# First norm through diagonal products: scaling and turning of x in one step, the samples' root apart, the first two projection units one after the other

## What is computed

```python
def rmsnorm(x, g):
    xf = x.astype(jnp.float32)
    y = xf * lax.rsqrt(jnp.mean(xf * xf, axis=-1, keepdims=True) + RMS_EPS) * g.astype(jnp.float32)
    return y.astype(x.dtype)
...
ap = rmsnorm(hp, norm_mix[i])
asm = rmsnorm(hs, norm_mix[i])
q, k, v, qi, ki, wi = attn_project(ap, pos_p, w_attn_in[j])
```

## Time and profile before

| | |
|---|---|
| median of 3 runs | 620.13 us (619.17 to 621.24) |
| profiled execution, span from first to last instruction | 619.9 us |
| mean granted TensorE clock | 0.992 |
| busy: TensorE / VectorE / ScalarE / GpSimd | 95% / 74% / 59% / 38% |

### The profile page before, as it was taken

How to read it: one execution, slowest core, us unless ns; L and a number is a source line. 1 busy time by engine, 2 the same in 40 slices (tenths; PEclk the granted TensorE clock), 3 DMA queues, 4 the chain that set the end, 5 groups by cost and what they waited for, 6 DMA issues and landing times.

```text
span 619.9 us, 12865 instructions
## 1 busy us (share of the span) xinstructions
PE 591.2 (95%) x5069; PEld 509.9 (82%) x5069; DVE 458.3 (74%) x900; ACT 366.8 (59%) x620; POOL 238.1 (38%) x259
## 2 busy tenths in 40 slices
PE   7889997899999999999999999898999999999995
PEld 6778875888888888888888778776888888888885
DVE  4779998465787777888668785888877788775442
ACT  6784555566576556666565687655765566653322
POOL 4222226642345445542000497923454454420000
PEclk9999999799999999999999999999999999999999
DMA  9678578235867666778997752035676667778501
GB/s 262 189 180 202 162 222 255 85 103 155 293 192 211 193 192 198 202 217 234 261 266 216 211 171 70 1 110 157 194 212 189 197 198 199 225 224 234 151 6 70
DMA packets 205421, 113.29 MB, mean 183 GB/s; under 512 B 5561, under 2 KB 202217, under 8 KB 205337
## 3 DMA queue, kind: packets, MB, share of 16 engines
q1 hardware_dynamic: 203169, 106.33, 60.7%
q0 software_dynamic: 1680, 5.79, 2.8%
q10 hardware_dynamic: 512, 0.35, 0.2%
HBM read 108.83 MB, written 3.86 MB: 182 GB/s over the span
## 4 chain that ended last, share of the span: by engine, by line
PE 66%; DVE 14%; POOL 7%; ACT 5%; issue 4%; DMA 3%; SPq 1%; DVEq 0%; POOLq 0%; ACTq 0%
PE acc L1467 18%; PE acc L1470 18%; PE acc L1473 18%; DVE w_lo L962 5%; PE acc L1447 2%; DMA stage<-in_w_ffn_down 2%; ACT w_hi L591 2%; POOL area L1954 1%; PE acc L1479 1%; DVE area L1094 1%; POOL area L1950 1%; POOL area L1959 1%; PE acc L1614 1%; POOL rtail L1949 1%; PE acc L1616 1%
## 5 line engine op out<-in xcount | busy, mean ns | idle before, releaser
L1467 PE MATMUL acc<-aH,w_hi 128*128 128x264 f16 (+1 forms) x904 | 250.0, 277 | 1.7 <-DVE aL L971 1.6
L1470 PE MATMUL acc<-aL,w_hi 128*128 128x264 f16 (+1 forms) x904 | 249.7, 276 | 0.0
L1473 PE MATMUL acc<-aH,w_lo 128*128 128x264 f16 (+1 forms) x904 | 249.7, 276 | 0.0
L962 DVE SCALAR_TENSOR_TENSOR w_lo<-stage,w_hi 128x1024 f16<-128x1024 f32 (+1 forms) x155 | 204.2, 1321 | 40.3 <-ACT w_hi L591 39.9
L591 ACT ACTIVATE w_hi<-stage 128x1024 f16<-128x1024 f32 (+1 forms) x155 | 171.4, 1109 | 38.4 <-PE acc L1473 27.5
L1467 PE MATMUL acc<-zH,w_hi 128*128 128x264 f16 x384 | 106.0, 276 | 0.0
L1470 PE MATMUL acc<-zL,w_hi 128*128 128x264 f16 x384 | 106.0, 276 | 0.0
L1473 PE MATMUL acc<-zH,w_lo 128*128 128x264 f16 x384 | 106.0, 276 | 0.0
L1467 PEld LDWEIGHTS acc<-aH,w_hi 128*128 128x128 f16 (+1 forms) x904 | 88.6, 98 | 16.0 <-DVE aL L971 2.2
L1470 PEld LDWEIGHTS acc<-aL,w_hi 128*128 128x128 f16 (+1 forms) x904 | 90.1, 100 | 13.6
L1473 PEld LDWEIGHTS acc<-aH,w_lo 128*128 128x128 f16 (+1 forms) x904 | 90.1, 100 | 12.9
(11 more groups left out here) (407 smaller groups left out, 969.5 us busy)
## 6 DMA issues: line engine op xcount, KB each, us to landing
stage<-in_w_ffn_up SPq DMA_DIRECT2D x88, 512.0 KB, 4.7
stage<-in_w_ffn_down SPq DMA_DIRECT2D x32, 704.0 KB, 6.1
stage<-in_w_attn_in SPq DMA_DIRECT2D x22, 512.0 KB, 6.0
stage<-in_w_rec_in SPq DMA_DIRECT2D x16, 512.0 KB, 4.8
stage<-in_w_attn_out SPq DMA_DIRECT2D x8, 512.0 KB, 3.9
stage<-in_w_rec_out SPq DMA_DIRECT2D x8, 512.0 KB, 3.8
area<-in_w_attn_in SPq DMA_DIRECT2D x4, 512.0 KB, 5.3
area<-in_x_prompt SPq DMA_DIRECT2D x2, 512.0 KB, 4.9
```

The costliest lines, as they stand in the source:

```text
L962: v.scalar_tensor_tensor(low, stage[:, place_in_line(u) % 4, 0:n, 0:cols], WSCALE, high, ALU.mult, ALU.subtract).then_inc(lo_done, 1)
L1467: t_.matmul(out, high[:, c, :], xH[:, x0 + c, :], start=first and c == 0, stop=False)
L1470: t_.matmul(out, high[:, c, :], xL[:, x0 + c, :], start=False, stop=False)
L1473: ins = t_.matmul(out, low[:, c, :], xH[:, x0 + c, :], start=False, stop=last and c == n - 1)
```

## The change

The row factors are no longer multiplied into the tokens. VectorE builds a diagonal matrix of them (`rdiag`, now at the start, and no longer at step 16), and TensorE multiplies a block of tokens by it, which scales and turns in one product; the transposes are gone. The samples' root, reciprocal and diagonal come ahead of the prompt's. The loads of the norm weights go from GpSimd's queue to ScalarE's, the loads of the page table and `blkc` the other way, and GpSimd sets `ones` ahead of its loads. `aH` of the samples is written by VectorE. Units 0 and 1 run one after the other, and `hi(1)` and `lo(1)` come after all eight chunks. The four warming products stand between the samples' and the prompt's products.

```diff
@@ ScalarE
-            act.dma_start(pt8[:], a["page_table"]).then_inc(pt_in, 16)
+            for i, name in enumerate(("norm_mix", "norm_ffn")):
+                act.dma_start(nrow[16 * i:16 * i + 16, :], a[name].rearrange("k (c p) -> (k c) p", p=P)).then_inc(nrm_in, 16)
+            act.dma_start(nrow[32:40, :], a["norm_final"].rearrange("(c p) -> c p", p=P)).then_inc(nrm_in, 16)
...
+            act.wait_ge(ss_act, 1)
+            nc.scalar.activation(rms[:, 2:3], ss[:, 2:3], ACT.Sqrt, bias=epsc[:, 0:1], scale=1.0 / D).then_inc(s_root, 1)
...
+            act.wait_ge(g_turned, 1)
+            nc.scalar.copy(gcol[:], acc[:, 2, 0:5 * DC]).then_inc(x_kept, 1)
...
-            nc.scalar.activation(rms[:], ss[:], ACT.Sqrt, bias=epsc[:, 0:1], scale=1.0 / D).then_inc(rms_root, 1)
-            act.wait_ge(r0tok_done, 1)
-            nc.scalar.activation(xtok[:, 0, :], xtok[:, 0, :], ACT.Copy, scale=r0tok[:, 0:1]).then_inc(xn0, 1)
+            nc.scalar.activation(rms[:, 0:2], ss[:, 0:2], ACT.Sqrt, bias=epsc[:, 0:1], scale=1.0 / D).then_inc(rms_root, 1)
...
@@ VectorE
+            dve.wait_ge(s_root, 1)
+            v.reciprocal(r0tok[:, 2:3], rms[:, 2:3]).then_inc(r0tok_done, 1)
...
+            v.tensor_scalar(rdiag[:, 2, :], ident, r0tok[:, 2:3], None, ALU.mult).then_inc(s_diag, 1)
...
-            v.tensor_scalar(xsmp, xsmp, r0tok[0:NS, 2:3], None, ALU.mult).then_inc(xn1, 1)
-            v.tensor_scalar(xtok[:, 1, :], xtok[:, 1, :], r0tok[:, 1:2], None, ALU.mult).then_inc(xn1, 1)
...
+            v.tensor_copy(aH[:, :, TP:T], xg[:]).then_inc(xg_done, 1)
+            dve.wait_ge(rms_root, 1)
+            v.reciprocal(r0tok[:, 0:2], rms[:, 0:2]).then_inc(r0tok_done, 1)
+            dve.wait_ge(r0tok_done, 2)
+            for t in range(2):
+                v.tensor_scalar(rdiag[:, t, :], ident, r0tok[:, t:t + 1], None, ALU.mult).then_inc(rdiag_done, 1)
...
@@ TensorE
+            t_.transpose(acc[:, 2, 0:5 * DC], nrow, ident[0:5 * DC, 0:5 * DC]).then_inc(g_turned, 1)
+            pe.wait_ge(s_diag, 1)
             for c in range(DC):
-                ins = t_.transpose(acc[:, 3, NS * c:NS * (c + 1)], xsmp[:, c * P:(c + 1) * P], ident[0:NS, 0:NS])
+                ins = t_.matmul(acc[:, 3, NS * c:NS * (c + 1)], xsmp[:, c * P:(c + 1) * P], rdiag[0:NS, 2, 0:NS], start=True, stop=True)
             ins.then_inc(s_turned, 1)
+            keep_warm(acc[:, 0, 0:P], WARM // 4)
             for c in range(DC):
+                for t in range(2):
+                    pe.wait_ge(rdiag_done, t + 1)
+                    ins = t_.matmul(misc[:, c // 2, c % 2 * TP + t * P:c % 2 * TP + (t + 1) * P], xtok[:, t, c * P:(c + 1) * P],
+                                    rdiag[:, t, :], start=True, stop=True)
                 if c % 2:
                     ins.then_inc(x_turned, 1)
...
-            keep_warm(acc[:, 2, 0:P], 4)
...
+            unit(0, aH, aL, ready=a_ready(0))
+            unit(1, aH, aL)
@@ GpSimd
-            for i, name in enumerate(("norm_mix", "norm_ffn")):
-                pool.dma_start(nrow[16 * i:16 * i + 16, :], a[name].rearrange("k (c p) -> (k c) p", p=P)).then_inc(nrm_in, 16)
-            pool.dma_start(nrow[32:40, :], a["norm_final"].rearrange("(c p) -> c p", p=P)).then_inc(nrm_in, 16)
             g.memset(ss[:], 1.0)
             g.memset(epsc[:], EPS)
+            g.memset(ones[:], 1.0).then_inc(ones_set, 1)
...
+            pool.dma_start(pt8[:], a["page_table"]).then_inc(pt_in, 16)
             g.memset(rfin[:], 1.0)
-            g.memset(ones[:], 1.0).then_inc(ones_set, 1)
```

More of the change, by code:

```diff
@@ L375, in build @@
         ss_act, ss_dve, r0tok_done = sem("ss_act"), sem("ss_dve"), sem("r0tok_done")
-        xn0, xn1, s_turned, x_turned = sem("xn0"), sem("xn1"), sem("s_turned"), sem("x_turned")
-        xg_done, xs_hi, x_kept = sem("xg_done"), sem("xs_hi"), sem("x_kept")
+        s_root, s_diag, g_turned, s_turned, x_turned = (sem(n) for n in ("s_root", "s_diag", "g_turned", "s_turned", "x_turned"))
+        xg_done, x_kept = sem("xg_done"), sem("x_kept")
         rdiag_done, r0_mm, r0_kept = sem("rdiag_done"), sem("r0_mm"), sem("r0_kept")
@@ L998, in _ @@
                                        aH[:, c, 0:TP], ALU.mult, ALU.subtract).then_inc(a_lo, 1)
-                if c == 3:
-                    lo(1)
+            lo(1)
             for u in (2, 3):
                 lo(u)
-            def turn_scales():
-                dve.wait_ge(const_in, 16)
-                for t in range(3):
-                    ins = v.tensor_scalar(rdiag[:, t, :], ident, r0tok[:, t:t + 1], None, ALU.mult)
-                ins.then_inc(rdiag_done, 1)
             def gate_params():
@@ L1631, in turn_rows @@
                 ins.then_inc(signal, 1)
-            keep_warm(acc[:, 2, 0:P], 4)
-            half = DC // 2
-            for c in range(DC):
-                a_ready(0)(c)
-                chunk(0, c, aH, aL)
-                if c >= half:
-                    chunk(1, 2 * (c - half), aH, aL)
-                    chunk(1, 2 * (c - half) + 1, aH, aL)
+            unit(0, aH, aL, ready=a_ready(0))
+            unit(1, aH, aL)
             for u in range(2, U_OUT + 1):
@@ L1707, in _ @@
                     pe.wait_ge(act_kept, DC + 4)
-                    pe.wait_ge(rdiag_done, 1)
                     for t in range(2):
@@ L1858, in scales @@
             def scales():
-                pool.wait_ge(r0tok_done, 1)
+                pool.wait_ge(r0tok_done, 2)
                 pool.wait_ge(r0_kept, 1)
```

38 lines of the change are left out of this document (13 added, 25 removed).

## The result

| | before | after |
|---|---|---|
| median | 621.39 us (619.17 to 627.65, 19 runs) | 627.27 us (623.84 to 633.10, 19 runs) |
| runs above 629 us | 0 of 19 | 8 of 19 |
| profiled execution: span / own time | 619.9 / not given | 629.9 / 631.76 us |

The changed kernel is slower: ratio 1.0106, 95% interval [1.0081, 1.0132], about 6 us. The prediction said 620.0 us within 618.6 to 621.6.

The account below looks back on a forecast made before the run. The chain to the end of `lo(2)`, then SyncE's queue to load 7, was taken to bound the kernel; `lo(2)` at 18.05 instead of 18.14 gave -0.1 us, span 619.8, median 620.0 us, range 618.6 to 621.6.

Parts of the forecast that it names:

- the path: First 20 us: the end of `lo(2)` (18.14 before) decides, through SyncE's queue, load 7 and ScalarE's restart.
- G: Start of the turning of the norm weights, once the last norm row lands: 8.05 us, bounds 7.5 to 8.5.
- rival 2: First norm: norm rows or samples' products later than the bounds; a landing at 9.3 gives +1.3 us, 621.3; chance 0.08.
- The samples' products: First norm: 8 products, 16 instructions, replace 8 transposes; 1.36 us, bounds 1.2 to 1.7.
- The prompt's products at 2.4 GHz: First norm: 16 products, 32 instructions at 0.111 us each, 3.55 us.
- rival 4: First norm: the prompt's products run at 1.2 GHz, 6.7 us instead of 3.55; +3.2 us, 623.2; chance 0.08.
- The four warming products: Ahead of the prompt's products: 0.89 us on TensorE, filling the 0.95 us in which VectorE makes the diagonals.
- S: Start of warming at about 1.6 us instead of 3.42, 1.8 us earlier, booked as a gain.
- Whatever moves 18.14 moves unit 7's load, ScalarE's restart and everything after it: From `lo(2)` to the end: its shift, -0.1 us (-0.8 to +0.7), passes one for one to the total.
- Rival 5: Low clock stretch at 108 to 115 us goes: 1.7 us, with an earlier part about 2.5, 617.4; chance 0.08.
- Units 0 and 1, queues, step 16: Unit order and load 5 hidden behind waits, page loads hidden, three fewer diagonals at step 16 (0.68 us): all at nothing.
- The base: Whole kernel: span 619.9 - 0.1 = 619.8, plus 0.2 us by which the median stood above it, 620.0.

Follow-up runs that it names:

- b_late7: Kernel before, with nine unused small loads on SyncE's queue ahead of load 7; ratio to before 1.0120, median 629.27 us.
- a_load7: Changed kernel, with load 7 issued ahead of the 21 small loads; 624.74 us, ratio to before 1.0036.
- b_diag: Kernel before, with only the diagonal products of the change; queues, late `ones` and woven units as before; 625.59 us, ratio to before 1.0020.
- a_late: Changed kernel, with `ones` set behind GpSimd's loads again; 629.95 us, ratio to before 1.0085.
- b_ones: Kernel before, with only `ones` set ahead of GpSimd's three loads; 621.93 us, ratio to before 1.0013.
- a_bridge: Changed kernel, with 24 warming products instead of 16 at the start; 627.18 us, ratio to before 1.0092.
- a_fill: Changed kernel, with ten warming products in TensorE's wait at step 23; 625.67 us, ratio to before 1.0048.
- a_queues: Changed kernel, with norm rows back on GpSimd's queue and page loads on ScalarE's, `ones` still first; 627.00 us, ratio to before 1.0061.
- b_load7: Kernel before, with load 7 issued ahead of the 21 small loads; 620.83 us, ratio to before 1.0003.
- a_woven: Changed kernel, with units 0 and 1 woven again and `hi(1)`, `lo(1)` behind the fourth chunk; 626.65 us, ratio to before 1.0061.
- b_queues: Kernel before, with only the exchange of the load queues and `ones` first; 621.52 us, ratio to before 0.9996.
- a_late_mend: Kernel before, with diagonal products, load 7 ahead of the small loads and ten filling products at step 23; 620.25 us, ratio to before 0.9984.
- b_mend: Kernel before, with load 7 ahead of the small loads and ten filling products at step 23; 619.47 us, ratio to before 0.9962.
- a_best: Changed kernel, with the queues of before, woven units, load 7 ahead of the small loads, ten filling products at step 23; 622.58 us.

## Why the prediction was wrong

**Right: the path.** That the end of `lo(2)` decides, by SyncE's queue, load 7 and ScalarE, is what b_late7 shows by itself and a_load7 from the other side: it took back 2.5 of the 5.9 us. Wrong were when `lo(2)` ends (21.30 instead of 18.05) and what that is worth.

**G, the norm rows (8.05, bounds 7.5 to 8.5).** It came at 9.18. The last row was issued at 2.99 instead of 2.7 and took 6.05 us instead of 5.3. In the six profiles whose chain shows its landing by ScalarE's queue it took 5.7 to 6.5 us; in the ten that issue it on GpSimd's, 5.2 to 5.6. The sum carried the 5.3 us of one queue over to the other. Its row for `ptc` (5.8 on ScalarE's queue) pointed the right way by luck: `ptc` takes 5.8 to 6.1 us by ScalarE's queue and 5.8 to 6.2 by GpSimd's. +1.1 us. The Trainium skill, DMA: Bandwidth & Descriptors, Latency and other measured facts, has the hardware queues 0.4 us quicker to the first byte. The profile doesn't show first bytes; the landings of the norm row go the other way here, and those of `ptc` show no difference. This and the next point are rival 2, which came true with +1.6 us where it had +1.3.

**The samples' products (1.36, bounds 1.2 to 1.7).** 1.88 in the chain, 0.117 us for each of 16 instructions. They are slower than the transposes of the same shape (0.074) and than the products with full weights (0.105) that were to bound them. It is the same in b_diag and a_late at the high clock. +0.5 us.

**The prompt's products at 2.4 GHz (3.55).** 4.95 in the chain: rival 4, which had a chance of 0.08. Its reason "the same warming stands here" failed: the same warming stood 2.4 us earlier, and a_late and b_ones show that this start is what goes with the fall. The other reason given, a wait for the norm rows, is not it (a_bridge). +1.4 us. The Trainium skill, TensorE: Matmul & The Clock Gate, What's actually happening, says that the clock follows how busy the array has recently been; a fall behind 3 us of unbroken work in a_bridge isn't explained by busy time alone, and what in the early start brings it stays open.

G, the samples and the clock are 3.05 of the 3.25 us by which `lo(2)` missed. The four warming products ahead of the prompt's add 0.3 us: 1.36 in the chain, 1.09 in a_late at the high clock, and 1.05 in the sum. Small differences behind them go the other way. These are the sizes in one profile; by the profile of a_fill `lo(2)` ended another 2 us later.

**S.** 1.06 instead of 1.6. It bought nothing: the warming was done at 6.8, and TensorE waited for the norm rows. The sum booked this start as a gain of 1.8 us, while its own G said that the norm rows bind. In a_late the warming ends at 8.7, and TensorE goes on to the norm rows at 8.79 without a wait for them.

**"Whatever moves 18.14 moves unit 7's load, ScalarE's restart and everything after it".** The prediction priced this one for one, +-0.8 us. That is the step that failed by most: in b_late7 a load 7 that is 2.9 us late cost 7 to 9 us. In after load 7 was 3.7 us late; TensorE's wait for `wrep` grew from 1.1 to 2.9 us, behind it came a low stretch that before didn't have, and at step 23 after was 5.1 us late.

**Rival 5, the low stretch at 108 to 115 us.** It was counted only as something to win. It can also grow: 13.7 us in after, 17.1 in b_late7, and the runs above 629 us of these kernels and of a_late have clocks of 0.975 to 0.981. All three profiled runs above 629 us (after, a_queues, b_late7) have a stretch of 13.7 us or more there; of the other nine without the filling only b_load7 has one of about that length (13.6 us). Such runs are 8 of 19 of after, 7 of 12 of a_late and 3 of 6 of b_late7, and none of before. The prediction had "the change shifts their phase only by tenths"; the shift was 5 us, and the price was not in the range at all.

**Units 0 and 1, queues, step 16.** Apart from G these were costed at nothing, and no run tells them from nothing: a_woven and a_queues are not told apart from after (the intervals overlap; with the low time taken out they stand 1.3 and 1.2 us below it, an estimate), b_queues is at 0.9996, and a_late_mend, which has the three diagonals at the start instead of at step 16, is not told apart from b_mend.

**The base.** The prediction set the profile's span against the median. Own times stand 1.8 us above spans, so the profiled execution was about 621.7, and more runs of before gave 621.4: 1.4 us of the miss of 7.3 (627.27 against 620.0).

**Open.** Why runs of one kernel fall into long and short ones; the low stretch behind step 23 is the largest part seen, but runs of before and after, taken one by one, have no trace that would tell. That a late load 7 brings long runs is shown; by which step between 45 and 110 us it does so is not. The 3.2 us that a_load7 leaves have no cause shown, and the total cost of b_diag is unclear.

## What to carry to other kernels

Before a microsecond at the start is priced one for one, look for the places later on where TensorE waits (here 1.1 us before `wrep` and 2.4 us at step 23): there a shift can turn into a low stretch of the clock. Ten filler products in the gap took away the runs above 629 us of the changed kernel (0 of 12, from 8 of 19), though not its whole loss. A load that later work waits for is safer ahead of twenty small ones: moving it gave back 2.5 us where it was late, and nothing where it wasn't. Work that is started earlier than its successor can use it buys nothing, and here it went with a loss of the clock; and a profile's span is compared with spans, not with the times of runs.

## What of the hardware was not expected

- An instruction of a 32-bit product with 8 weight rows and 8 columns takes 0.117 us at the high clock, no less than one with 128 x 128 (0.111); the transpose of that shape takes 0.074.
- The clock fell to 1.2 GHz while TensorE was busy without a gap (a_bridge at 13 us, a_best at 10.5 us), and stayed there for 12 us of unbroken work (after, 116 to 128 us).
- The last norm row, 4 KB, landed 0.7 us later from ScalarE's queue than from GpSimd's (6.05 in after against 5.35 in a_queues); `ptc`, 0.5 KB, landed in 6.0 us from either (after, a_queues).
- Nine loads of some 1.4 KB each, which nothing uses, ahead of a load that ScalarE waits for, made a kernel of 621 us 7 to 9 us slower (b_late7).
